# Middle stages of a hybrid encoder step: the low parts of weight blocks cut on VectorE, the query norm sums placed inside the projection, and the third norm's transposes placed between output products

## The chip, the cores and the metric

The kernel runs on one core of one Trainium2 chip. The metric is the device time of one execution in microseconds (us). Three runs of the kernel before took 1071.44, 1071.8 and 1072.5 us; their median is 1071.8 us. TensorE (PE) multiplies, VectorE (DVE), ScalarE (ACT) and GpSimd (POOL) do the rest, and SyncE (SP) issues all DMAs.

## The reference, cut to what matters

One layer runs for 640 tokens: a prompt of 512 and eight samples of 16. The change touches the end of the mixer, the memory cross-attention and the start of the ConvFFN.

```python
x = x + jnp.concatenate([y_a, y_b, y_c], axis=-1) @ w_mix_out

h = rmsnorm(x, norm_mem_g)
qm = rmsnorm((h @ w_mq).reshape(B, T, MEM_HEADS, MEM_DH), mq_norm_g)
s = jnp.einsum('bthd,bnhd->bhtn', qm, mem_k) * (MEM_DH ** -0.5)
p = jax.nn.softmax(s, axis=-1)
om = jnp.einsum('bhtn,bnhd->bthd', p, mem_v).reshape(B, T, MEM_W)
x = x + om @ w_mo

h = rmsnorm(x, norm_ffn_g)
gt, ffn_buf_new = causal_dwconv(h @ w_gate, ffn_buf, ffn_conv_w)
x = x + (jax.nn.silu(gt) * (h @ w_up)) @ w_down
```

The memory's keys and values of the prompt come from `m = rmsnorm(mem)`, `m @ w_mk` and `m @ w_mv`; those of the samples are read from caches. D_MODEL is 1024, MEM_HEADS 4, MEM_DH 128, 256 memory rows, D_FF 2816.

## The kernel before, in words

All engines run programs written out by hand, each strictly in its order, and wait for each other on semaphores. Tokens are cut into five tiles of 128 rows (`NT` = 5); tile 4 (`PT`) holds the samples.

**Products in three parts.** A large product multiplies a high and a low part: high weight by high activation, high by low, low by high. Weights come in blocks of 1 MB (128 x 2048 numbers), numbered in the order of their use: 16 and 17 the second half of `w_mix_out`, 18 and 19 `w_mk`, 20 and 21 `w_mq`, 22 and 23 `w_mv`, 24 and 25 `w_mo`, then `w_gate` (26, 28, ...) and `w_up` (27, 29, ...) in turn. `load_w(i)` on SP brings block i into `wraw[i % 3]` once block i-3 is used up (`passed`). `cut_hi(i)` on ACT copies it into `whi[i % 2]` once block i-2 is used up. `cut_lo(i)` writes the low part over `wraw`; it stands in the program of VectorE (line 1808) or of GpSimd (line 1210), as `on_dve(i)` says, and `lo_cut` is PE's wait for it. Before the change GpSimd cuts blocks 19 and 21 to 27 of the middle stages.

**Norms.** For tile n, ACT sums squares (`square_rows`, line 1636) and forms the root, VectorE scales the rows (`scaled_rows`, line 2156) into one of two buffers `xn`, PE transposes them (`turn_rows`, line 505), ACT copies the high part (`norm_hi`, line 1335) and VectorE the low part (`norm_lo`, line 1818).

**Memory attention.** The two query blocks give `qm`; four heads' squares (`q_square`, line 2204) are summed by PE with a matrix of ones (line 924), ACT forms the roots, VectorE scales (line 2209). For each tile i PE forms the scores (`mem_scores`, line 938; `sample_scores`, line 976, for the samples), VectorE the maxima (`soft_max`, lines 2220 and 2223), ACT the exponentials (line 1696), VectorE divides by the sums (`soft_norm`, lines 2228 and 2230), PE transposes (`mem_probs`, line 948), ACT copies out, PE multiplies by the values (`mem_values`, line 961; `sample_values`, line 991), ACT and VectorE split the result (`om_part`), PE multiplies by `w_mo` (`mem_out`, lines 487 to 489), VectorE adds to the residual (`add_mem`, line 2149). PE's loop staggers these:

```python
for i in range(NT):
    if i + 1 < PT:
        mem_scores(i + 1)
    elif i + 1 == PT:
        sample_scores()
    if i == 0:
        memory_rows("mv", B_MV, 1, mv_banks)
    mem_probs(i)
    if i >= 1:
        mem_values(i - 1)
    if i >= 2:
        mem_out(i - 2)
```

PE writes into eight PSUM banks taken in a ring (`take`); a bank is taken again only when its reader has freed it. In this loop the scores of tile 2 take the two banks of the `w_mv` product.

The FFN starts with `across_half`, lines 420 to 422: the first gate block on tokens 0 to 319, then the last transposes, the first up block, and both on tokens 320 to 639.

## Time and profile before

| what | value |
|---|---|
| median of three runs | 1071.8 us |
| time of the profiled execution | 1075.18 us |
| its span (first to last instruction) | 1073.5 us |
| busy: PE, DVE, ACT, POOL | 1020.7, 534.2, 393.6, 117.3 us |
| PE idle from 400 to 640 us of the span, sum of the listed waits | 20.1 us |
| TensorE clock granted, mean | 0.984 |

The busy time of PE overlaps its own pipelining, so its share says only that PE rarely waits. All waits of PE from 400 to 640 us of the span lie between 463 and 606 us: these are the stages that the change edits. The granted clock is a share of 2.4 GHz; 0.50 is the lower level, 1.2 GHz.

### The profile page before, as it was taken

What the parts mean: (1) busy time and instruction counts of PE and PEld (TensorE: products, weight loads), DVE (VectorE), ACT (ScalarE), POOL (GpSimd) and SP (SyncE); (2) the same over time, 40 slices, a digit from 0 to 9 for tenths busy, and PEclk for the clock granted to TensorE, in tenths of its full rate; (3) what the DMA queues carried; (4) which work ended last, traced back from release to release, by engine and by line L of the source; (5) the groups of instructions that cost most, each with busy time, mean ns of one, the idle gap of its engine ahead of it and who ended that gap; (6) DMA issues with size and microseconds to landing.
All of it is one profiled execution on the core that took longest, in us unless ns stands there. A gap on an engine that the chain in (4) does not pass through costs nothing.

```text
span 1073.5 us, 16639 instructions
## 1 busy us (share of the span) xinstructions
PE 1020.7 (95%) x7027; PEld 913.8 (85%) x7027; DVE 534.2 (50%) x944; ACT 393.6 (37%) x729; POOL 117.3 (11%) x118
## 2 busy tenths in 40 slices
PE   4999999999999979989889799999999999999998
PEld 3888888897888857869678799999999999888887
DVE  5323686775756463662553444444444445533531
ACT  5413344438633434443544422222222223433320
POOL 0500000000373332013310300000000000000000
PEclk8999999999999989999989899999999999999999
DMA  7342233121101234342631222211222222212231
GB/s 265 124 151 89 79 118 119 41 81 44 40 2 52 70 126 158 107 138 98 230 104 59 79 80 79 77 61 64 77 79 79 79 80 86 79 59 79 79 108 49
DMA packets 73513, 98.44 MB, mean 92 GB/s; under 512 B 2528, under 2 KB 53856, under 8 KB 73312
## 3 DMA queue, kind: packets, MB, share of 16 engines
q1 hardware_dynamic: 73440, 97.39, 27.4%
q8 instruction: 56, 0.92, 0.4%
q14 instruction: 17, 0.14, 0.0%
HBM read 89.65 MB, written 7.73 MB: 91 GB/s over the span
## 4 chain that ended last, share of the span: by engine, by line
PE 82%; DVE 9%; ACT 5%; POOL 2%; issue 2%; DMA 0%; SPq 0%; DVEq 0%; ACTq 0%
PE bank L402 30%; PE bank L461 6%; PE bank L463 6%; PE bank L462 6%; PE bank L434 3%; PE bank L436 3%; PE bank L435 3%; PE bank L487 2%; PE bank L489 2%; PE bank L488 2%; PE bank L712 1%; DVE wlo L1808 1%; PE bank L516 1%; PE bank L420 1%; POOL lmb L1281 1%
## 5 line engine op out<-in xcount | busy, mean ns | idle before, releaser
L402 PE MATMUL bank<-hhi,whi 128*128 128x320 f32 x736 | 221.7, 309 | 0.1
L402 PE MATMUL bank<-hlo,whi 128*128 128x320 f32 x736 | 221.6, 309 | 0.0
L1325 ACT ACTIVATE whi<-wraw 128x2048 fp32r<-128x2048 f32 (+1 forms) x59 | 111.4, 1888 | 188.5 <-PE bank L402 95.8
L402 PE MATMUL bank<-hhi,wlo 128*128 128x320 f32 x736 | 167.6, 309 | 0.0
L1808 DVE TENSOR_TENSOR wlo<-wraw,whi 128x2048 fp32r<-128x2048 f32 (+1 forms) x50 | 112.3, 2246 | 89.5 <-ACT whi L1325 89.5
L402 PEld LDWEIGHTS bank<-hhi,whi 128*128 128x128 f32 x736 | 138.2, 188 | 0.4 <-issue 0.3
L402 PEld LDWEIGHTS bank<-hlo,whi 128*128 128x128 f32 x736 | 138.1, 188 | 0.1
L402 PEld LDWEIGHTS bank<-hhi,wlo 128*128 128x128 f32 x736 | 123.0, 188 | 0.0
L434 PE MATMUL bank<-hhi,whi 128*128 128x320 f32 x352 | 114.2, 324 | 0.7 <-DVE gT L1861 0.7
L436 PE MATMUL bank<-hhi,wlo 128*128 128x320 f32 x352 | 108.8, 309 | 0.0
L435 PE MATMUL bank<-hlo,whi 128*128 128x320 f32 x352 | 108.7, 309 | 0.0
L461 PE MATMUL bank<-whi,hhi 128*128 128x512 f32 x200 | 79.1, 396 | 6.2 <-DVE hlo L1827 6.2
L462 PE MATMUL bank<-wlo,hhi 128*128 128x512 f32 x200 | 78.8, 394 | 0.0
L463 PE MATMUL bank<-whi,hlo 128*128 128x512 f32 x200 | 78.8, 394 | 0.0
L434 PEld LDWEIGHTS bank<-hhi,whi 128*128 128x128 f32 x352 | 66.2, 188 | 4.0 <-issue 3.7
L1374 ACT ACTIVATE cb<-bank 128x320 f32<-128x320 f32 x34 | 14.9, 438 | 147.7 <-PE bank L402 110.0
L435 PEld LDWEIGHTS bank<-hlo,whi 128*128 128x128 f32 x352 | 66.2, 188 | 1.7 <-issue 1.4
L436 PEld LDWEIGHTS bank<-hhi,wlo 128*128 128x128 f32 x352 | 66.1, 188 | 0.0
L1210 POOL TENSOR_TENSOR wlo<-wraw,whi 128x2048 fp32r<-128x2048 f32 x10 | 45.8, 4586 | 147.7 <-ACT whi L1325 147.7
L2308 DVE TENSOR_TENSOR act<-act,bank 128x320 f32<-128x320 f32 x44 | 19.5, 484 | 71.1 <-PE bank L402 71.1
L461 PEld LDWEIGHTS bank<-whi,hhi 128*128 128x128 f32 x200 | 38.2, 191 | 14.6 <-issue 6.7
L1868 DVE COPY fcst<-cb 128x2 f32<-128x2 f32 x22 | 3.7, 170 | 83.5 <-ACT cb L1377 83.3
(369 smaller groups left out, 1800.4 us busy)
## 6 DMA issues: line engine op xcount, KB each, us to landing
wraw<-in_w_in SPq DMA_DIRECT2D x14, 1024.0 KB, 5.3
wraw<-in_w_gate SPq DMA_DIRECT2D x11, 1024.0 KB, 5.2
wraw<-in_w_up SPq DMA_DIRECT2D x11, 1024.0 KB, 5.3
wraw<-in_w_down SPq DMA_DIRECT2D x10, 1024.0 KB, 5.0
kTs<-in_cache_sb_k SPq DMA_DIRECT2D x8, 512.0 KB, 5.4
vraw<-in_cache_sb_v SPq DMA_DIRECT2D x8, 512.0 KB, 6.0
wraw<-in_w_mix_out SPq DMA_DIRECT2D x4, 1024.0 KB, 5.0
kmT<-in_cache_mem_k SPq DMA_DIRECT2D x8, 512.0 KB, 5.8
```

The source lines that it names most:

```text
L402: ins = T.matmul(bank[bs[h]][:, 0:HALF], w[:, k, c * P:(c + 1) * P], a[:, k, h * HALF:(h + 1) * HALF], start=(k == 0 and w is wh and a is hi),
L434: T.matmul(o, wh[:, k, cs], hhi[:, k, hs], start=(k == 0), stop=False)
L435: T.matmul(o, wh[:, k, cs], hlo[:, k, hs], start=False, stop=False)
L436: ins = T.matmul(o, wl[:, k, cs], hhi[:, k, hs], start=False, stop=(k == KD - 1))
L461: T.matmul(o, hi[:, t * P:(t + 1) * P], wh[:, kk, :], start=(k == 0), stop=False)
L462: T.matmul(o, hi[:, t * P:(t + 1) * P], wl[:, kk, :], start=False, stop=False)
L463: ins = T.matmul(o, lo[:, t * P:(t + 1) * P], wh[:, kk, :], start=False, stop=(k == nk - 1))
L487: T.matmul(bank[b][:, :], hi[:, tt], wh[:, kk, :], start=(k + kk == 0), stop=False)
L488: T.matmul(bank[b][:, :], hi[:, tt], wl[:, kk, :], start=False, stop=False)
L1210: G.tensor_tensor(wv(wlo, i), wv(wraw, i), wv(whi, i).bitcast(F32), ALU.subtract)\
L1325: V(wv(whi, i), wv(wraw, i), ACT.Copy).then_inc(s["w_hi_ready"], 1)
L1808: V.tensor_tensor(wv(wlo, i), wv(wraw, i), wv(whi, i).bitcast(F32), ALU.subtract)\
```

## The change

- All weight blocks from 16 on are cut on VectorE; GpSimd keeps blocks 14 and 15 only, and takes over the clearing of the two tiles `pz` from VectorE.
- Both `w_mk` blocks are cut before tile 4 of the second norm is squared and scaled.
- The query norm sums of heads 0 and 1 stand between the two halves of the second query block, that of head 2 behind it, and that of head 3 inside the first `w_mv` product.
- VectorE, not ACT, scales the memory values out of PSUM (`memv`).
- The first gate block (26) gets a high buffer of its own, `whi_gate`, in the place of two of the samples' key tiles; it is loaded before the last of the samples' value tiles and cut in iteration 3 of the loop.
- The third norm's transposes stand between output products; the output product of tile 4 is split into its two column halves.

```diff
         def on_dve(i):
-            return i < B_OUT[0][0] or i in B_OUT[1] or i in (B_MK[0], B_MQ[0]) or i >= B_GU[1][0]
+            return i not in B_OUT[0]
...
+            if t is whi and i == B_GU[0][0]:
+                return whi_gate[:, :].rearrange("p (k c) -> p k c", k=nk)
...
-            across(("mq", 1), B_MQ[1], hhi, hlo)
+            across(("mq", 1), B_MQ[1], hhi, hlo, cs=(0,))
...
+            query_sums(0)
+            query_sums(1)
+            across(("mq", 1), B_MQ[1], hhi, hlo, cs=(1,))
+            query_sums(2)
...
+            memory_rows("mv", B_MV, 0, mv_banks, behind=lambda kk: query_sums(3) if kk == 0 else None)
...
             sample_values()
+            turn_norm3(0)
+            turn_sample_values()
             mem_out(3)
-            turn_norm3(0)
             turn_norm3(1)
-            turn_sample_values()
+            mem_out(PT, 0)
             turn_norm3(2)
-            mem_out(PT)
+            mem_out(PT, 1)
             turn_norm3(3)
...
+            load_w(B_GU[0][0])
             filled(sp, ("ms", PT, 1))
             load_mem_v(7)
-            for i in range(B_GU[0][0], B_DN[0][0] + 2):
+            for i in range(B_GU[0][1], B_DN[0][0] + 2):
...
-            for i in range(B_MK[1], B_GU[1][0]):
-                if i != B_MQ[0]:
-                    cut_lo(i)
+            passed(pool, B_MV[1])
+            for n in range(2):
+                ins = G.memset(pz[n][:, :, :, :], 0.0)
+            ins.then_inc(s["pz_ready"], 1)
...
-                if i == 0:
-                    for t in range(2):
-                        b = filled(e, ("mv", 0, t))
-                        V(memv[:, t, :], bank[b][:, :], ACT.Copy, scale=stat[:, 2, t:t + 1]).then_inc(bank_free[b], 1)
-                    cut_hi(B_MO[1][0])
...
+                if i == 3:
+                    cut_hi(B_GU[0][0])
...
+            cut_lo(B_MV[1])
             soft_max(0)
+            cut_lo(B_MO[0][0])
             soft_norm(0)
...
+                        for t in range(2):
+                            b = filled(dve, ("mv", 0, t))
+                            V.tensor_scalar(memv[:, t, :], bank[b][:, :], stat[:, 2, t:t + 1], None, ALU.mult)\
+                                .then_inc(bank_free[b], 1)
...
+                if i == 3:
+                    cut_lo(B_GU[0][0])
```

On PE, behind the second query block, the program before has the transposes of the memory keys, then the sums of the four heads in a row (`sqM`), then the first `w_mv` product:

```order
L402 MATMUL bank<-hhi,wlo_173 128x320 x2
L918 MATMUL bank<-ident,mkout 128x128 x8
L924 MATMUL bank<-sqM_166,ones 128x320 x2
L924 MATMUL bank<-sqM_167,ones 128x320 x2
L924 MATMUL bank<-sqM_166,ones 128x320 x2
L924 MATMUL bank<-sqM_167,ones 128x320 x2
L895 MATMUL bank<-whi_176,mhi 128x512
```

In the changed program the same place of PE reads as follows; the rows left out are the second half of the query block (39 rows) and the first six rows of the `w_mv` product:

```order
L923 MATMUL bank<-ident,mkout 128x128 x8
L930 MATMUL bank<-sqM_166,ones 128x320 x2
L930 MATMUL bank<-sqM_167,ones 128x320 x2
L405 MATMUL bank<-hhi,whi_178 128x320
...
L405 MATMUL bank<-hhi,wlo_173 128x320 x2
L930 MATMUL bank<-sqM_166,ones 128x320 x2
L898 MATMUL bank<-whi_177,mhi 128x512
...
L930 MATMUL bank<-sqM_167,ones 128x320 x2
L898 MATMUL bank<-whi_177,mhi 128x512
```

Two heads' sums have moved ahead of half a query block, and one behind a quarter of the next product. On VectorE, from the copies of the samples' queries (`qz`) to the second tile's softmax, before:

```order
L2241 COPY qz_200<-qm 128x16x16
L2220 TENSOR_REDUCE mstat<-bank 128x2 x2
L2223 TENSOR_SCALAR mstat<-mstat 128x4
L2228 RECIPROCAL mstat<-mstat 128x4
L2230 TENSOR_SCALAR probs_195<-probs_195,mstat 128x256 x4
L2220 TENSOR_REDUCE mstat<-bank 128x2 x2
L2223 TENSOR_SCALAR mstat<-mstat 128x4
L2228 RECIPROCAL mstat<-mstat 128x4
```

And in the changed program, on the same engine and at the same place:

```order
L2263 COPY qz_201<-qm 128x16x16
L1828 TENSOR_TENSOR wlo_175<-wraw_172,whi_178 128x2048
L2242 TENSOR_REDUCE mstat<-bank 128x2 x2
L2245 TENSOR_SCALAR mstat<-mstat 128x4
L1828 TENSOR_TENSOR wlo_173<-wraw_170,whi_177 128x2048
L2250 RECIPROCAL mstat<-mstat 128x4
L2252 TENSOR_SCALAR probs_196<-probs_196,mstat 128x256 x4
L2242 TENSOR_REDUCE mstat<-bank 128x2 x2
L2245 TENSOR_SCALAR mstat<-mstat 128x4
L2279 TENSOR_SCALAR memv<-bank,stat 128x512 x2
L2250 RECIPROCAL mstat<-mstat 128x4
```

Two cuts (`wlo`) and the scaling of the memory values have come into the softmax chain of VectorE. On SP's DMA queue, from the seventh of the samples' value tiles on, before:

```order
L1156 DMA mkraw_135<-in_cache_mem_v 128x2x512
L1169 DMA out_p_mem_v<-memv 128x2x512
L1156 DMA mkraw_136<-in_cache_mem_v 128x2x512
L1067 DMA wraw_172<-in_w_gate 128x8x256
L1067 DMA wraw_170<-in_w_up 128x8x256
```

The same stretch of SP's queue in the changed program:

```order
L1169 DMA mkraw_135<-in_cache_mem_v 128x2x512
L1182 DMA out_p_mem_v<-memv 128x2x512
L1080 DMA wraw_172<-in_w_gate 128x8x256
L1169 DMA mkraw_136<-in_cache_mem_v 128x2x512
L1080 DMA wraw_170<-in_w_up 128x8x256
```

The first gate block has passed the last value tile, and with it the wait for the samples' scores.

## Rows read from the trace of the kernel before

**Rows 1.** The page: busy time of the engines, and DMA time to landing

```profile
PE 1020.7 (95%) x7027; PEld 913.8 (85%) x7027; DVE 534.2 (50%) x944; ACT 393.6 (37%) x729; POOL 117.3 (11%) x118
...
wraw<-in_w_up SPq DMA_DIRECT2D x11, 1024.0 KB, 5.3
```

**Rows 2.** PE's waits, 400 to 640 us: total, times, longest

```profile
PE bank L948 <- DVE probs L2230: 3.8, 2, 2.4
PE bank L924 <- DVE sqM L2204: 2.2, 2, 2.0
```

**Rows 3.** Stretches: busy us (instructions) per engine, PE clock, DMA share, GB/s

```profile
474.40:482.30 7.90, 7.90 (x33) 6.77 (x34) 4.65 (x5) 3.00 (x3) 0.00 (x0) 0.80 0.22 87
523.90:553.00 29.10, 22.45 (x113) 19.27 (x112) 19.31 (x30) 13.16 (x34) 11.49 (x3) 0.88 0.61 217
605.10:612.00 6.90, 6.87 (x30) 6.90 (x31) 2.17 (x5) 1.83 (x4) 4.78 (x1) 0.60 0.09 27
```

**Rows 4.** Timeline of PE, 470 to 606 us: start, duration, idle before

```profile
474.40 1.97 PE L505 MATMUL bank<-ident,xn 128*128 128x128 f32 x8 [4.09 <-DVE xn L2156]
...
523.87 3.61 PE L938 MATMUL bank<-memkT,qm 128*128 128x256 f32 x16
527.13 0.58 PE L895 MATMUL bank<-whi,mhi 128*128 128x512 f32 x1
...
538.32 3.16 PE L938 MATMUL bank<-memkT,qm 128*128 128x256 f32 x8 [2.85 <-ACT memv L1728]
...
553.00 0.47 PE L487 MATMUL bank<-whi,omhi 128*128 128x512 f32 x1
...
562.25 1.09 PE L948 MATMUL bank<-ident,probs 128*128 128x128 f32 x8
563.18 1.95 PE L961 MATMUL bank<-probT,memv 128*128 128x128 f32 x16
564.89 0.47 PE L487 MATMUL bank<-whi,omhi 128*128 128x512 f32 x1
...
570.47 1.04 PE L948 MATMUL bank<-ident,probs 128*128 128x128 f32 x8
...
578.67 3.70 PE L991 MATMUL bank<-mkraw,pz 128*32 128x128 f32 x128
...
592.83 1.28 PE L505 MATMUL bank<-ident,xn 128*128 128x128 f32 x8 [2.60 <-DVE xn L2156]
...
605.13 0.61 PE L420 MATMUL bank<-hhi,whi 128*128 128x320 f32 x1 [3.27 <-POOL wlo L1210]
```

**Rows 5.** Timeline of POOL: a memset, and two stretches of cuts

```profile
342.86 0.95 POOL L1288 MEMSET apart_w<- 128x1024 f32 x1 [17.85 <-PE bank L436]
...
468.73 4.53 POOL L1210 TENSOR_TENSOR wlo<-wraw,whi 128x2048 fp32r<-128x2048 f32 x1 [39.57 <-ACT whi L1325]
...
521.76 9.11 POOL L1210 TENSOR_TENSOR wlo<-wraw,whi 128x2048 fp32r<-128x2048 f32 x2 [16.71 <-ACT whi L1325]
```

**Rows 6.** Timeline of DVE, 459 to 543 us

```profile
459.11 1.28 DVE L2156 SCALAR_TENSOR_TENSOR xn<-xres,stat,gmem 128x1024 f32<-128x1024 f32 x1 [1.90 <-issue]
...
462.15 2.29 DVE L1808 TENSOR_TENSOR wlo<-wraw,whi 128x2048 fp32r<-128x2048 f32 x1 [0.56 <-ACT whi L1325]
...
470.37 3.98 DVE L2156 SCALAR_TENSOR_TENSOR xn<-xres,stat,gmem 128x1024 f32<-128x1024 f32 x1
...
526.52 4.38 DVE L2223 TENSOR_SCALAR mstat<-mstat 128x4 f32<-128x4 f32 x1
...
533.18 1.14 DVE L2230 TENSOR_SCALAR probs<-probs,mstat 128x256 f32<-128x256 f32 x4
534.23 1.28 DVE L2220 TENSOR_REDUCE mstat<-bank 128x2 f32<-128x512 f32 x2
535.55 0.17 DVE L2223 TENSOR_SCALAR mstat<-mstat 128x4 f32<-128x4 f32 x1
...
542.24 3.02 DVE L2223 TENSOR_SCALAR mstat<-mstat 128x4 f32<-128x4 f32 x1
```

**Rows 7.** Timeline of ACT: the second w_mk block's high part

```profile
466.75 1.90 ACT L1325 ACTIVATE whi<-wraw 128x2048 fp32r<-128x2048 f32 x1
```

More of the change, by code:

```diff
@@ L885, in _, with memory_rows @@
             pe.wait_ge(s["mem_lo"], 1)
-            def memory_rows(name, blks, part, bs):
+            def memory_rows(name, blks, part, bs, behind=lambda kk: None):
                 lo_cut(pe, blks[part])
@@ L899, in memory_rows @@
                             done(ins, (name, 0, t))
+                    if kk < 3:
+                        behind(kk)
                 if part == 0:
@@ L1000, in turn_sample_values, with mem_out @@
                 done(ins, ("om", PT))
-            def mem_out(n):
+            def mem_out(n, *halves):
                 evacuated(pe, ("om", n))
-                for half in range(2):
+                for half in halves or range(2):
                     rows_tiles("mo", half, B_MO[half], lambda h, k: (omhi[:, k, :], omlo[:, k, :]), (n,))
@@ L1668, in _, with query_roots @@
             cut_hi(B_MV[0])
[L1669 to L1675 removed]
+            def query_roots(h):
                 if h >= 2:
@@ L2257, in _ @@
                 if i == 1:
-                    passed(dve, B_MV[1])
-                    for n in range(2):
-                        ins = V.memset(pz[n][:, :, :, :], 0.0)
-                    ins.then_inc(s["pz_ready"], 1)
+                    cut_lo(B_MO[1][0])
                 if i == 2:
```

51 lines of the change are left out of this document (32 added, 19 removed).

## Prediction

> **What bounds the kernel now.** I read the page first: PE is busy 95% of the span, VectorE 50% and GpSimd 11% [rows 1]. So time can be won only where PE waits or where its clock is down, and a few us of extra work on VectorE cost nothing unless PE waits for them. The view of PE's waits says where that is: from 400 to 640 us it idles 20.1 us, all between 463 and 606. The timeline of PE places the waits. There are four places. Before the last transposes of the second norm PE stands 4.09 us [rows 4]. Within the query norm sums it stands 2.2 us [rows 2]. Between the first scores (523.87) and the first output product (553.00) it stands twice for normalised probabilities, 3.8 us together [rows 2], and 2.85 us for the banks of the memory values [rows 4]. Before the FFN it stands 2.60 us for scaled rows and 3.27 us for the cut of the gate block [rows 4]. The stretches show the second part of the price: after each of these, the granted clock is below 1, so that some of the matmuls run at 1.2 instead of 2.4 GHz: 0.80 over 7.9 us, 0.88 over 29.1 us, 0.60 over 6.9 us [rows 3]. PE had stood still before each fall.
>
> The timelines of VectorE and GpSimd name the cause of most of it. A cut takes 2.29 us on VectorE [rows 6] and 4.53 us on GpSimd [rows 5]. And while GpSimd cuts, VectorE's instructions between SBUF tiles stand: the scaled rows take 3.98 us at 470.37, where 1.28 is normal, and the four numbers of `mstat` take 4.38 and 3.02 us, where 0.17 is normal [rows 6]. Each overlaps a GpSimd cut: 468.73 to 473.26, and 521.76 to 530.87 [rows 5].
>
> **The change part by part.**
>
> *Second norm, last tile.* The load of the second `w_mk` block lands at 466.75, when ACT starts on its high part, done at 468.65 [rows 7]. Now ACT does that before the squares of tile 4, and VectorE cuts for 2.29 us, to about 470.95, then scales for 1.28 us, to about 472.3. Today the transposes start at 474.40: 2.1 us won. Idle of about 2.0 us stays, because the squares now queue behind the load. What the clock does then is open. If it stays up, the 7.9 us at 0.80 give back up to 7.9 x 0.20 = 1.6 us; if not, nothing. I take the middle, 0.8. The first query block's cut, next on VectorE, then ends some 0.5 us before PE asks for it, because its high part waits on ACT behind both halves of this norm.
>
> *Query norm sums.* Heads 0 and 1 are squared long before the half block that now follows them; heads 2 and 3 have half a projection (7 us, a quarter of the 28 us that both blocks take) and 1.4 us of the `w_mv` product as cover. The 2.2 us of waiting go [rows 2]. Without the cover they would be back. The work is the same number of matmuls.
>
> *From the first scores to the first output product.* Today 29.13 us pass (523.87 to 553.00). The work at full clock, from start to start of rows: two tiles' scores 3.26 (523.87 to 527.13), a product of 24 matmuls 5.58 (564.89 to 570.47), three rounds of transposes of 0.93 (562.25 to 563.18), two of values of 1.71 (563.18 to 564.89), two more tiles of scores 3.26, in sum 18.3 us [rows 4]. So if nothing waited, 10.8 us would go. Does VectorE keep up? In these 18.3 us it has three maxima (1.28 + 0.17), three divisions (0.18 + 1.14) [rows 6], two evacuations of `memv` of 0.68, one low part of 0.69, and about three cuts of 2.29: some 17 us, 90% full. Going step by step from the first scores: scores in PSUM at 1.8 us, VectorE free of the `w_mv` cut at 1.6, maxima at 3.3, exponentials 1.9 us, `w_mo` cut beside them to 5.5, probabilities at 6.9; PE is in the `w_mv` product until 9.1, so this round is covered by 2 us. `memv` is scaled at 9.9, just when PE asks for those banks after its transposes. Second probabilities at 11.7 against PE's 11.6; third at 16.5 against 16.0; the second `w_mo` cut is done at 21.0 against 21.9. I leave 0.6 us for the two thin ones: 10.2 us won. Of that, 6.65 us is idle time and the rest is clock.
>
> *Clearing `pz` on GpSimd.* Two memsets of about 0.95 us [rows 5], released by the end of the `w_mv` product, beside the second tile's division. They take 1.8 us off VectorE. Nothing in the trace shows a memset beside that work. Bounds: nothing, and 1.9 us if they hold VectorE as the cuts do. A memset reads no SBUF tile, so it is nearer to nothing; I take 0.3. The Trainium skill, "SBUF — State Buffer", section "Who interferes with whom", has one exclusive port pair for GpSimd and VectorE's two-port forms, whoever comes first, for the whole instruction, `tensor_scalar` among them. By that rule the memsets could hold the division for up to their length, which is the upper bound above; the rows on cuts agree with it.
>
> *Before the FFN.* Today 26.46 us pass from the samples' values (578.67) to the first gate matmul (605.13). The work: 3.7 for the values, four transposes of 0.93, 0.5 for the turned sample values, two output products of 5.58, in sum 19.1 us [rows 4]; so 7.4 us go if nothing waits. Going through: scaled rows 0 and 1 are ready before the loop's end, row 2 about 5 us before its turn, row 3 about 2 us. The gate block, loaded from about 10 us after the first scores, is cut some 20 us before its use. The up block is loaded when the first half of tile 4's output product ends, lands 5.3 us later [rows 1], and is cut after the last scaled rows, 10.3 us after its issue; PE reaches it after 12.4 us. It is covered by 2 us. The first half of the gate block runs at 0.60 today for 6.9 us: 2.8 us come back, since no idle precedes it [rows 3].
>
> Sum: 2.1 + 0.8 + 2.2 + 10.2 - 0.3 + 7.4 + 2.8 = 25.2 us. The FFN behind is the same stream, so all of it should reach the end. The profiled execution took 1075.18 us, span 1073.5, and should take about 1050.0. It lay 3.4 us above the median of 1071.8, which I take as what the profile adds to both; so 1071.8 - 25.2 = **1046.6 us**.
>
> **The rivals.**
>
> *VectorE becomes the bound in the softmax loop.* Every cut stands between a maximum and a division or ahead of a maximum. If the handovers take longer than I set, three cuts (6.9 us) and `memv` (1.4) come onto PE's path, and the clock stays down as today (about 3.5 us). For it: 90% full, covers of 0.1 and 0.5 us. Against it: VectorE's 19.31 busy us of that stretch hold 7.1 us of standing for GpSimd (4.38 + 3.02 less 2 x 0.17) [rows 3, 6]. It would give 1046.6 + 11.8 = 1058 us. Chance 0.13.
>
> *The waits shrink but the clock is not given back, or the up block comes late.* A 2 us hole remains at the second norm, behind a 0.9 us one; short waits of 0.5 to 1 us at the third and fourth probabilities could keep the clock down as in the 29 us today. Loses 3.5 + 0.8, or for the up block 1 to 3 us and part of the 2.8: about 1051 to 1053. Chance 0.16.
>
> *Slower than before.* The gate block's high part waits on ACT in iteration 3, ahead of the samples' transposed probabilities, for its load and for the samples' scores. If that load came late, everything on ACT stood behind it: the probabilities' copies, the third tile's `om_part`, and so PE. It would have to be more than 30 us late to eat the gain and the cover (it is issued some 18 us before the wait, with 5.3 us to land [rows 1]). Delays of that size give over 1075. Chance 0.02.
>
> *The change does nothing here.* The waits would have to reappear at full size behind other causes, in a kernel with VectorE at 50%: within 0.2% of before, 1070 to 1074. Chance 0.01.
>
> *More than I sum.* Clock at full everywhere and the second norm's idle gone: 20.1 us of waits and 10 us of clock, 1041.7. Chance 0.04 beyond 1043.
>
> **How the numbers follow.** The forecast, 1043 to 1049.5, has 0.64. With the case of the clock it reaches 1053, in sum 0.80, so the range is 1042 to 1054; the rest lies mostly above. 0.2% (2.1 us) is about what a measurement can tell from no change. Every case but two, which hold 0.03, is faster; I leave a little more for what I have not seen: faster 0.95, same 0.02, slower 0.03.
>
> **What would show it.** In the changed profile: no GpSimd cut after 400 us; `xn` never above 1.3 us and `mstat` at 0.17; transposes of the second norm about 2 us earlier; no wait at the sums; first scores to first output product in about 19 us, at a clock near 1; no wait of PE on the gate block, and its first half at 0.147 us a matmul. I am wrong if PE waits for `probs`, `memv` or `wlo` for more than 2 us in sum in that stretch, if the division shows a stall beside the memsets, or if the FFN that follows grows.

## The result

The changed kernel took 1047.16 us in the median of four runs (1045.9 to 1048.69). Four runs of the kernel before had a median of 1072.15 us (1071.44 to 1074.93). The ratio is 0.9757, with a 95% interval of 0.9731 to 0.9783: the kernel is 2.4% faster. 1046.6 was predicted.

The page of the changed kernel, its span, busy times and granted clock per slice, answers to [rows 1]:

```profile
span 1046.6 us, 16640 instructions
...
PE 1011.6 (97%) x7027; PEld 907.0 (87%) x7027; DVE 538.9 (51%) x952; ACT 392.0 (37%) x727; POOL 82.3 (8%) x112
...
PEclk8999999999999998999999999999999999999999
```

PE is busy 9 us less although it issues the same 7027 matmuls: they run at the higher clock. GpSimd loses 35 us, VectorE gains only 5. The eight cuts it took over are 18 us of work (8 x 2.29), and it no longer stands while GpSimd cuts: behind the change its scaled rows take 1.27 to 1.28 us and the four numbers of `mstat` 0.17. The waits of PE from 400 to 640 us (total, times, longest), which answer to [rows 2], were 20.1 us before and are now 2.3. One of them lies outside the stages that the change edits, 0.36 us at 429.22 before and 0.33 at 430.25 now (`mxlo`), so 19.7 us, not 20.1, lay between 463 and 606.

```profile
PE bank L898 <- DVE wlo L1828: 0.9, 1, 0.9
PE bank L508 <- DVE xn L2176: 0.6, 1, 0.6
PE bank L960 <- DVE probs L2252: 0.5, 2, 0.3
PE bank L464 <- POOL mxlo L1317: 0.3, 1, 0.3
```

Stretches, with the columns of [rows 3]; the last three figures of a row are PE's clock, the DMA share and GB/s. The first row is the whole loop from the first scores to the first output product. The clock was 0.88 in that loop before and is 1.00 now.

```profile
517.19:536.61 19.42, 18.92 (x114) 16.39 (x112) 15.35 (x30) 11.93 (x31) 1.84 (x2) 1.00 0.89 301
...
460.00:480.00 20.00, 18.51 (x93) 15.28 (x93) 14.61 (x14) 11.63 (x15) 0.00 (x0) 1.00 0.53 185
...
580.00:600.00 20.00, 20.00 (x142) 19.99 (x141) 6.95 (x10) 6.74 (x13) 0.00 (x0) 1.00 0.21 71
```

The places of [rows 4] on PE's timeline now:

```profile
465.60 0.47 PE L898 MATMUL bank<-whi,mhi 128*128 128x512 f32 x1 [0.88 <-DVE wlo L1828]
...
471.93 1.09 PE L508 MATMUL bank<-ident,xn 128*128 128x128 f32 x8 [0.61 <-DVE xn L2176]
...
517.19 3.61 PE L950 MATMUL bank<-memkT,qm 128*128 128x256 f32 x16
...
529.15 1.09 PE L960 MATMUL bank<-ident,probs 128*128 128x128 f32 x8 [0.28 <-DVE probs L2252]
...
533.97 1.09 PE L960 MATMUL bank<-ident,probs 128*128 128x128 f32 x8 [0.22 <-DVE probs L2252]
...
536.61 0.48 PE L490 MATMUL bank<-whi,omhi 128*128 128x512 f32 x1
...
580.80 0.39 PE L423 MATMUL bank<-hhi,whi_gate 128*128 128x320 f32 x1
```

No wait stands before the first gate matmul (580.80). Cut into stages by the start of their first matmul, each difference below is one of two such rows. The kernels of the next section, most of which take parts of the change back, are in the same table, so that each part can be read in its own column. The last column is the rest of the span behind the first gate matmul; since that half block runs first there, the clock at the gate shows in it.

| kernel | first `w_mk` to first query block | to key transposes | to first scores | to first output product | to sample values | to first gate matmul | all six | rest of the span |
|---|---|---|---|---|---|---|---|---|
| before | 17.70 | 28.15 | 13.43 | 29.13 | 25.67 | 26.46 | 140.54 | 468.37 |
| changed | 12.74 | 21.12 | 17.73 | 19.42 | 25.65 | 18.54 | 115.20 | 465.80 |
| e1_cuts_alone | 16.32 | 28.15 | 14.56 | 20.00 | 25.65 | 23.90 | 128.58 | 466.26 |
| e2_cuts_back | 16.59 | 21.11 | 17.74 | 21.64 | 26.83 | 18.53 | 122.44 | 466.42 |
| e3_sums_back | 12.57 | 28.17 | 14.85 | 19.42 | 25.65 | 18.53 | 119.19 | 465.85 |
| e4_gate_late | 12.54 | 21.13 | 17.73 | 19.42 | 25.66 | 20.23 | 116.71 | 466.33 |
| e5_turns_back | 12.62 | 21.12 | 17.73 | 19.42 | 25.65 | 22.98 | 119.52 | 465.81 |
| e6_memv_act | 12.79 | 21.12 | 17.73 | 19.42 | 25.67 | 18.53 | 115.26 | 465.82 |
| e7_pz_vector | 12.72 | 21.13 | 17.74 | 18.72 | 25.65 | 18.54 | 114.50 | 465.87 |
| e8_pz_later | 12.85 | 21.12 | 17.73 | 19.80 | 25.66 | 18.54 | 115.70 | 465.89 |
| e9_squares_first | 12.00 | 21.11 | 17.74 | 19.41 | 25.66 | 18.53 | 114.45 | 465.85 |
| e10_pz_at_cut | 13.15 | 21.11 | 17.74 | 18.72 | 25.65 | 18.54 | 114.91 | 465.86 |
| e11_pool_busy | 12.92 | 21.13 | 17.74 | 25.01 | 25.66 | 18.53 | 120.99 | 465.85 |
| e12_both | 12.06 | 21.12 | 17.73 | 18.72 | 25.66 | 18.53 | 113.82 | 465.84 |

From the second column on, stages that an edit doesn't touch repeat within 0.03 us (the last column within 0.1), so this table tells apart what the run times, with their 1 to 3 us of scatter, don't. It rests on one profiled execution of each kernel. The first column scatters by 0.6 where it isn't edited (12.54 to 13.15). Moved work must be seen in it: half a query block (7 us) left the second column for the third in the changed kernel.

### The profile page after: what moved, and what is told of

Read it like the earlier page. It is cut to its first block, busy times and chain, and to the rows that moved or that the text cites. A ratio compares the mean times of both kernels' runs of the same rounds, so it can differ in the third digit from the quotient of the medians.

```text
span 1046.6 us, 16640 instructions
## 1 busy us (share of the span) xinstructions
PE 1011.6 (97%) x7027; PEld 907.0 (87%) x7027; DVE 538.9 (51%) x952; ACT 392.0 (37%) x727; POOL 82.3 (8%) x112
## 3 DMA queue, kind: packets, MB, share of 16 engines
q1 hardware_dynamic: 73440, 97.39, 27.9%
## 4 chain that ended last, share of the span: by engine, by line
PE 84%; DVE 7%; ACT 4%; POOL 2%; issue 1%; DMA 1%; SPq 0%; DVEq 0%; ACTq 0%
PE bank L405 31%; PE bank L464 6%; PE bank L465 6%; PE bank L466 6%; PE bank L437 4%; PE bank L439 3%; PE bank L438 3%; PE bank L492 2%; PE bank L490 2%; PE bank L491 2%; PE bank L715 1%; DVE wlo L1828 1%; PE bank L519 1%; POOL lmb L1295 1%; PE bank L423 1%
## 5 line engine op out<-in xcount | busy, mean ns | idle before, releaser
L1828 DVE TENSOR_TENSOR wlo<-wraw,whi 128x2048 fp32r<-128x2048 f32 (+1 forms) x57 | 128.4, 2252 | 95.8 <-ACT whi L1342 95.8
L465 PEld LDWEIGHTS bank<-wlo,hhi 128*128 128x128 f32 x200 | 38.3, 191 | 7.9
```

The lines of the kernel that those rows point to most:

```text
L465: T.matmul(o, hi[:, t * P:(t + 1) * P], wl[:, kk, :], start=False, stop=False)
L1828: V.tensor_tensor(wv(wlo, i), wv(wraw, i), wv(whi, i).bitcast(F32), ALU.subtract)\
```

## The experiments

The run times, each beside runs of the kernel before on the same chip:

| kernel | median, us | ratio to before | 95% interval |
|---|---|---|---|
| e1_cuts_alone | 1061.18 | 0.9875 | 0.9835 to 0.9915 |
| e2_cuts_back | 1054.79 | 0.9817 | 0.9769 to 0.9866 |
| e3_sums_back | 1050.40 | 0.9777 | 0.9737 to 0.9817 |
| e4_gate_late | 1049.25 | 0.9763 | 0.9722 to 0.9803 |
| e5_turns_back | 1051.62 | 0.9809 | 0.9794 to 0.9824 |
| e6_memv_act | 1046.48 | 0.9765 | 0.9751 to 0.9780 |
| e7_pz_vector | 1046.42 | 0.9765 | 0.9750 to 0.9780 |
| e8_pz_later | 1047.07 | 0.9770 | 0.9753 to 0.9786 |
| e9_squares_first | 1046.44 | 0.9764 | 0.9749 to 0.9778 |
| e10_pz_at_cut | 1045.68 | 0.9757 | 0.9741 to 0.9774 |
| e11_pool_busy | 1052.12 | 0.9818 | 0.9803 to 0.9832 |
| e12_both | 1045.98 | 0.9760 | 0.9746 to 0.9775 |

The theory: each stage had its own wait, on its own cause, and each part of the change removes one; the cuts on VectorE take away GpSimd's holding of VectorE, and the orders take away the rest. The rivals: that one part does nearly all of it, and that VectorE, or the clock, is the bound in the softmax loop after all.

**The cuts alone (e1_cuts_alone).** The kernel before, with the cuts on VectorE at places that fit its order, and nothing else.

```diff
         def on_dve(i):
-            return i < B_OUT[0][0] or i in B_OUT[1] or i in (B_MK[0], B_MQ[0]) or i >= B_GU[1][0]
+            return i not in B_OUT[0]
...
-            for i in range(B_MK[1], B_GU[1][0]):
-                if i != B_MQ[0]:
-                    cut_lo(i)
...
                 scaled_rows("norm2", n, 7, gmem, xn2)
+                if n == PT:
+                    cut_lo(B_MK[1])
...
+            cut_lo(B_MV[1])
             soft_max(0)
+            cut_lo(B_MO[0][0])
             soft_norm(0)
...
             norm_lo("norm3", 2)
+            cut_lo(B_GU[0][0])
             add_mem(4)
```

> The kernel before with one part of the change alone: all cuts of blocks 19 and 21 to 27 on VectorE, none on GpSimd; PE's order, the norm sums, memv on ScalarE and the place of the gate block's load and high part are as before. Theory (the slow and blocking cuts on GpSimd were the main cost): second norm 2 us earlier, the VectorE instructions that stood 2.7 to 4.2 us stand no more, so the stretch from the first scores to the first output product shrinks by about 8 us, the gate block's wait of 3.3 us to about 1, some clock comes back; gain 12 to 16 us, about 1058 us. Rival (the placement of PE's work and the early gate block pay, the cuts only ride along): gain under 6 us, over 1066 us.

It took 1061.18 us. The six stages shrink by 11.96 us and the rest of the span by 2.11, just under the 12 to 16 us that I expected. Its four largest waits of PE:

```profile
PE bank L505 <- DVE xn L2153: 4.0, 2, 2.6
PE bank L895 <- DVE wlo L1805: 2.0, 2, 1.1
PE bank L924 <- DVE sqM L2204: 2.0, 1, 2.0
PE bank L420 <- DVE wlo L1805: 1.0, 1, 1.0
```

The loop falls to 20.00 by the cuts alone. The waits for the sums (`sqM`) and for scaled rows (`xn`, 1.4 and 2.6) stay, and the clock falls behind them. So the cuts alone are worth about half of the whole; the other half needs the orders.

**All but the cuts (e2_cuts_back).** The changed kernel with GpSimd cutting the blocks it cut before, and `pz` cleared on VectorE.

```diff
         def on_dve(i):
-            return i not in B_OUT[0]
+            return i < B_OUT[0][0] or i in B_OUT[1] or i in (B_MK[0], B_MQ[0]) or i >= B_GU[1][0]
...
-            passed(pool, B_MV[1])
-            for n in range(2):
-                ins = G.memset(pz[n][:, :, :, :], 0.0)
-            ins.then_inc(s["pz_ready"], 1)
+            for i in range(B_MK[1], B_GU[1][0]):
+                if i != B_MQ[0]:
+                    cut_lo(i)
```

> The changed kernel with the cuts of blocks 19 and 21 to 27 given back to GpSimd, in the same order as before, and pz cleared on VectorE; everything else stays changed (norm sums, transposes, gate buffer, memv on VectorE). Theory: the stalls of VectorE come back (xn and mstat at 3 to 4.4 us), loss of 12 to 16 us against the changed kernel, about 1060 us, all of it before the first output product; the stretch before the FFN stays short, since the early gate block hides even a 4.5 us cut. Rival: loss under 5 us, below 1052 us.

It took 1054.79 us: 18.10 us off the six stages and 1.95 off the rest. Against the changed kernel it loses 7.2 us in the stages, where I had expected 12 to 16, and 1.18 of it lies behind the first output product, where I had expected none. Neither my theory nor its rival (a loss under 5 us) had the size. VectorE's and then GpSimd's timeline show the holding once more:

```profile
525.69 3.20 DVE L2247 TENSOR_SCALAR probs<-probs,mstat 128x256 f32<-128x256 f32 x4
...
560.65 4.58 DVE L2175 SCALAR_TENSOR_TENSOR xn<-xres,stat,gffn 128x1024 f32<-128x1024 f32 x1
```

```profile
518.84 9.10 POOL L1224 TENSOR_TENSOR wlo<-wraw,whi 128x2048 fp32r<-128x2048 f32 x2 [13.55 <-ACT whi L1341]
...
559.57 4.57 POOL L1224 TENSOR_TENSOR wlo<-wraw,whi_gate 128x2048 fp32r<-128x2048 f32 x1 [14.59 <-ACT whi_gate L1341]
```

A division takes 3.20 for 1.14, scaled rows 4.58 for 1.28. In the loop that costs only 2.2 us more than on VectorE (21.64 against 19.42), and the clock is 1.00 there (523 to 545 us). That the new order has more cover is my reading; no run takes its parts there one by one. The halves don't simply add: 11.96 and 18.10 make 30.1, where both together give 25.34. In the loop they overlap, since the cuts alone win 9.13, the rest alone 7.49 and both 9.71. In the second norm they need each other: 1.38 and 1.11 alone, 4.96 together. The first rival falls, except in the loop, where either half does most of it.

**The sums back together (e3_sums_back).**

```diff
-            across(("mq", 1), B_MQ[1], hhi, hlo, cs=(0,))
+            across(("mq", 1), B_MQ[1], hhi, hlo)
...
-            query_sums(0)
-            query_sums(1)
-            across(("mq", 1), B_MQ[1], hhi, hlo, cs=(1,))
-            query_sums(2)
-            for g in range(2):
-                take(("mqn", 3, g))
+            for h in range(HEADS):
+                query_sums(h)
...
-            memory_rows("mv", B_MV, 0, mv_banks, behind=lambda kk: query_sums(3) if kk == 0 else None)
+            memory_rows("mv", B_MV, 0, mv_banks)
```

> The changed kernel with the four heads' query norm sums back in a row behind the whole second query block, on PE and on ScalarE. Theory: PE waits again for the squares of heads 2 and 3, 2.0 to 2.5 us in sum, and the clock stays at 1 there as it did before: 1049 to 1050 us. Rival (the sums were no cost because a later wait would swallow them): 1047 us and a wait further on that shrinks by as much.

It took 1050.40 us. The second and third column together are 43.02 against 38.85, 4.17 us more; the six stages 3.99. PE's timeline, then the stretch around it:

```profile
509.15 1.37 PE L930 MATMUL bank<-sqM,ones 128*128 128x320 f32 x4 [1.96 <-DVE sqM L2220]
...
510.75 2.50 PE L930 MATMUL bank<-sqM,ones 128*128 128x320 f32 x4 [0.23 <-DVE sqM L2220]
```

```profile
509.00:515.00 6.00, 5.62 (x16) 3.81 (x16) 2.96 (x5) 4.01 (x8) 0.00 (x0) 0.72 0.58 231
```

The 2.2 us of [rows 2] are back (1.96 + 0.23), and here the clock fell behind them, to 0.72. In the kernel before it had stayed up at the same place after the same wait. That is most of the other 2 us (0.28 x 6.0 = 1.7), and it is what I had not expected: I had the clock stay up, as before.

**The gate block late (e4_gate_late).** Block 26 without a high buffer of its own: loaded behind the last value tile, and cut behind the scaled rows.

```diff
             _, nk, n = blocks[i]
-            if t is whi and i == B_GU[0][0]:
-                return whi_gate[:, :].rearrange("p (k c) -> p k c", k=nk)
...
-            load_w(B_GU[0][0])
             filled(sp, ("ms", PT, 1))
             load_mem_v(7)
-            for i in range(B_GU[0][1], B_DN[0][0] + 2):
+            for i in range(B_GU[0][0], B_DN[0][0] + 2):
...
             norm_lo("norm3", 2)
+            cut_lo(B_GU[0][0])
             add_mem(4)
```

> The changed kernel without the gate block's own buffer and early cuts: load behind the samples' last value tile, high part after the first half of tile 4's output product, low part next on VectorE. The transposes between output products stay. Theory: PE waits about 1.5 to 2 us for the low part before the first gate matmul; whether the clock falls after so short a wait decides between a loss of 2 us (1049) and of up to 5 us (1052). Rival (the gate wait was only GpSimd's slowness): no wait, 1047 us.

It took 1049.25 us. The last stage is 1.69 longer and the rest 0.53. PE waits 1.45 at the gate, and the clock stays up. PE's timeline, and the stretch from there:

```profile
581.37 0.38 PE L421 MATMUL bank<-hhi,whi 128*128 128x320 f32 x1 [1.45 <-DVE wlo L1822]
```

```profile
581.30:590.00 8.70, 8.60 (x58) 8.19 (x59) 6.15 (x9) 6.02 (x11) 0.00 (x0) 1.00 0.27 93
```

So the early gate block is worth some 1.7 us once the cut is on VectorE (2.2 with the 0.53 behind it, whose cause wasn't looked for). The 3.27 us wait of [rows 4] was for GpSimd's cut; with the cut on VectorE, in the order before, it is 1.00 (e1).

**The transposes back (e5_turns_back).** The order of the kernel before between the output products, with the third tile's addition on VectorE where that order needs it.

```diff
             sample_values()
-            turn_norm3(0)
-            turn_sample_values()
             mem_out(3)
+            turn_norm3(0)
             turn_norm3(1)
-            mem_out(PT, 0)
+            turn_sample_values()
             turn_norm3(2)
-            mem_out(PT, 1)
+            mem_out(PT)
             turn_norm3(3)
```

> The changed kernel with the third norm's transposes and the samples' values in their old places behind tile 3's output product, and that of tile 4 in one piece; VectorE's order there as before; the gate block stays early. Theory: PE waits about 2.6 us for the scaled rows of tile 2 and the clock falls behind it as before (0.84 over 14.9 us): loss of 3 to 5 us, 1050 to 1052 us. Rival (the wait was caused by what stood before it and is gone with it): 1047 us.

It took 1051.62 us; the last stage is 22.98, 4.44 more. PE's timeline and the stretch behind that wait:

```profile
575.57 1.09 PE L508 MATMUL bank<-ident,xn 128*128 128x128 f32 x8 [2.60 <-DVE xn L2175]
```

```profile
575.50:590.00 14.50, 14.43 (x78) 12.96 (x79) 7.89 (x10) 6.55 (x14) 0.00 (x0) 0.88 0.46 146
```

It is the 2.60 us wait of [rows 4], with GpSimd doing nothing. That wait was a matter of order, as VectorE's timeline shows:

```profile
571.88 1.29 DVE L1837 TENSOR_TENSOR hlo<-bank,hhi 128x512 fp32r<-128x512 f32 x2 [0.38 <-ACT hhi L1351]
573.63 0.69 DVE L2258 TENSOR_TENSOR omlo<-bank,omhi 128x512 fp32r<-128x512 f32 x1 [0.46 <-ACT omhi L1732]
574.24 1.27 DVE L2175 SCALAR_TENSOR_TENSOR xn<-xres,stat,gffn 128x1024 f32<-128x1024 f32 x1
```

The rows that PE waits for are those of tile 2 (`turn_norm3(2)`). Their addition and their root were done by 564.0. But on VectorE their scaling stands behind the low part of tile 0 and that of the samples' output, and both of these need transposes that PE reaches only at 570.62 and 572.36, just ahead. In the changed kernel PE transposes tile 0 right behind the samples' values, and tile 2 is scaled 7.4 us before its turn (569.02 and 576.39). The clock fell behind the wait (0.88 over 14.5 us, 1.7 us).

**The memory values on ACT again (e6_memv_act).** This takes 1.4 us off VectorE in the loop. If VectorE were the bound, PE should gain by it.

```diff
+                if i == 0:
+                    for t in range(2):
+                        b = filled(e, ("mv", 0, t))
+                        V(memv[:, t, :], bank[b][:, :], ACT.Copy, scale=stat[:, 2, t:t + 1]).then_inc(bank_free[b], 1)
...
-                    if i == 0:
-                        for t in range(2):
-                            b = filled(dve, ("mv", 0, t))
-                            V.tensor_scalar(memv[:, t, :], bank[b][:, :], stat[:, 2, t:t + 1], None, ALU.mult)\
-                                .then_inc(bank_free[b], 1)
```

> The changed kernel with the memory values scaled out of PSUM by ScalarE again. Theory: ScalarE comes to them only after the second tile's exponentials and then to the transposed probabilities 1.2 us later; PE waits 0.7 to 1.5 us for the two banks, VectorE is 1.4 us freer; 1047.5 to 1048.5 us. Rival (VectorE at 90% is the bound in this loop): the 1.4 us taken off VectorE make it faster, 1046 us or less.

The loop takes 19.42 us, as with it on VectorE, and the run 1046.48. PE now waits 0.4 for `memv` and no longer for `probs` (0.5 before). So where the values are scaled makes no difference in the new order. I had expected a wait of 0.7 to 1.5 us and a loss; and since one wait takes the place of another, this run alone doesn't test whether VectorE is the bound.

**`pz` cleared on VectorE (e7_pz_vector).** Now VectorE has 1.8 us more to do, and GpSimd nothing.

```diff
-            passed(pool, B_MV[1])
-            for n in range(2):
-                ins = G.memset(pz[n][:, :, :, :], 0.0)
-            ins.then_inc(s["pz_ready"], 1)
...
                     cut_lo(B_MO[1][0])
+                    passed(dve, B_MV[1])
+                    for n in range(2):
+                        ins = V.memset(pz[n][:, :, :, :], 0.0)
+                    ins.then_inc(s["pz_ready"], 1)
```

> The changed kernel with pz cleared on VectorE (1.8 us) behind the second w_mo cut, none on GpSimd. Theory (the memsets on GpSimd held VectorE's division for 0.7 us): the second division is back at 1.14 us, PE's wait of 0.28 us before the second transposes goes; the 1.8 us on VectorE are covered; time within 0.5 us of the changed kernel. Rival (VectorE is the bound): the 1.8 us show on PE ahead of the fourth transposes.

The loop is shorter: 18.72 us, and both waits for `probs` are gone. VectorE's own memsets come at 535.74, 1.6 us behind the loop's end (534.17), and the stage there is no longer for them (25.65 us). VectorE's and GpSimd's timelines of the changed kernel show why the loop is shorter:

```profile
522.42 1.14 DVE L2252 TENSOR_SCALAR probs<-probs,mstat 128x256 f32<-128x256 f32 x4
...
527.24 1.85 DVE L2252 TENSOR_SCALAR probs<-probs,mstat 128x256 f32<-128x256 f32 x4
```

```profile
526.33 1.84 POOL L1321 MEMSET pz<- 128x1024 f32 x2 [96.14 <-PE bank L900]
```

The second division overlaps the memsets (526.33 to 528.17) and takes 0.71 us longer than the first. In e7 the same division takes 1.15. So the memsets cost the loop 0.70 us. In run time that isn't told apart from nothing: 1046.42 against 1047.16, with intervals that overlap.

**The memsets elsewhere (e8_pz_later, e10_pz_at_cut).** Both were meant to bring the memsets beside a cut on VectorE, to see whether they hold that too. In e8 they wait for the first memory values' product, in e10 for its evacuation.

```diff
             passed(pool, B_MV[1])
+            filled(pool, ("om", 0))
             for n in range(2):
```

```diff
             passed(pool, B_MV[1])
+            evacuated(pool, ("om", 0))
             for n in range(2):
```

> The changed kernel with GpSimd's two memsets held until the first output tile of the attention is in PSUM, beside VectorE's second w_mo cut (a subtraction of two SBUF tiles). If a memset on GpSimd holds only VectorE's one-input scalings, the cut stays at 2.29 us, the second division is back at 1.14 us and PE's 0.28 us wait goes; if it holds any work between SBUF tiles, the cut takes 3 to 4 us or the memsets wait for it. Time within 0.5 us of the changed kernel either way.

> The changed kernel with GpSimd's two memsets released when VectorE has freed the first output tile's bank, so that they run beside VectorE's second w_mo cut (two SBUF inputs), not beside a scaling. If memsets hold only VectorE's one-input scalings, the cut starts at once after its high part and lasts 2.29 us, and no scaling is stretched; if they hold the cut too, it lasts or waits 1 to 2 us longer. PE's wait of 0.28 us before the second transposes goes in both cases; time 1046 to 1047 us.

In e8 the product ended earlier than I had placed it, and the memsets fell on the third division, so it didn't test what I had written down; e10 does. GpSimd's row, then VectorE's, then PE's:

```profile
529.37 1.99 POOL L1322 MEMSET pz<- 128x1024 f32 x2 [101.61 <-PE bank L973]
```

```profile
529.80 2.22 DVE L2253 TENSOR_SCALAR probs<-probs,mstat 128x256 f32<-128x256 f32 x4
```

```profile
532.07 1.09 PE L960 MATMUL bank<-ident,probs 128*128 128x128 f32 x8 [1.10 <-DVE probs L2253]
```

The third division takes 2.22, PE waits 1.10 for it, and the loop is 19.80, 1.08 more than without memsets there. In e10 they met the cut, GpSimd's row and VectorE's:

```profile
532.51 1.84 POOL L1322 MEMSET pz<- 128x1024 f32 x2 [104.30 <-DVE omlo L2260]
```

```profile
533.50 2.29 DVE L1829 TENSOR_TENSOR wlo<-wraw,whi 128x2048 fp32r<-128x2048 f32 x1 [1.11 <-ACT whi L1343]
```

The cut takes its 2.29 and the loop 18.72, as without memsets. So in these runs memsets held VectorE's scaling of one SBUF tile and not its subtraction of two. The Trainium skill, "SBUF — State Buffer", section "Who interferes with whom", says the same: an instruction of VectorE with two SBUF inputs contends only with one of GpSimd that reads SBUF, while `tensor_scalar` in its two-port form contends with any. By that rule the price of the memsets hangs on which instruction they meet, and e7, e8 and e10 bear it out with 0.70, 1.08 and 0.

**GpSimd made busy (e11_pool_busy).** Four multiplications in which GpSimd reads SBUF, placed in the loop; nothing reads what they write, and nothing of the computation is left out.

```diff
+            for i in (B_MV[1], B_MO[0][0]):
+                pool.wait_ge(s["w_hi_ready"], i + 1)
+                for n in range(2):
+                    link(G.tensor_tensor(lmask[:, :, :], lmask[:, :, :], lmask[:, :, :], ALU.mult))
             passed(pool, B_MV[1])
```

> The changed kernel, all cuts on VectorE in time, with four added multiplications on GpSimd of two SBUF tiles of 128 x 896 (about 2 us each by the 4.53 us for 2048 columns), two released by the high part of block 23 and two by that of block 24; nothing reads their results. It takes the lateness of GpSimd's cuts away and leaves only their holding of VectorE. If holding is the larger part of what the cuts cost in the softmax loop, VectorE's instructions stretch by 4 to 8 us in sum and the loop from the first scores to the first output product grows from 19.4 by 2 us or more. Rival (lateness was the cost): the loop stays within 0.5 us of 19.4.

It took 1052.12 us, and the loop 25.01, 5.59 more. GpSimd's timeline, first the four in one row, then three of them by themselves; then VectorE's:

```profile
515.10 11.06 POOL L1322 TENSOR_TENSOR lmask<-lmask 128x896 f32<-128x896 f32 x4 [86.45 <-ACT whi L1346]
...
515.10 3.79 POOL L1322 TENSOR_TENSOR lmask<-lmask 128x896 f32<-128x896 f32 x1 [86.45 <-ACT whi L1346]
518.96 3.68 POOL L1322 TENSOR_TENSOR lmask<-lmask 128x896 f32<-128x896 f32 x1
522.72 1.68 POOL L1322 TENSOR_TENSOR lmask<-lmask 128x896 f32<-128x896 f32 x1
```

```profile
518.82 2.28 DVE L1832 TENSOR_TENSOR wlo<-wraw,whi 128x2048 fp32r<-128x2048 f32 x1
...
521.23 6.11 DVE L2256 TENSOR_SCALAR probs<-probs,mstat 128x256 f32<-128x256 f32 x4
```

The division stands for 5 us (6.11 for 1.14) with GpSimd's multiplications, which lie on nobody's path. The cut at 518.82 isn't stretched, though GpSimd's four lie across it: there GpSimd stood. Its third and fourth multiplications take 1.68 us each, its first two 3.79 and 3.68, and each of these two began 0.05 and 0.14 us behind the start of a cut on VectorE (515.05 and 518.82, 2.29 and 2.28 us). The Trainium skill, "SBUF — State Buffer", section "Who interferes with whom", has the shared ports as an exclusive lock, which for VectorE's two-port forms whoever issues first keeps for its whole instruction. The held division agrees with it (6.11 us), and here the two cuts, which have two SBUF inputs, held GpSimd in the same way. So the holding alone, with no cut moved, lengthens the loop by 5.6 us, part of it as clock (0.66 over 526 to 536 us). That is what these four cost in the new order, not a share of the 9.7 us of the change: GpSimd's real cuts cost 2.2 in the same loop (e2).

**Squares first (e9_squares_first).** In the second norm ACT and VectorE take tile 4's squares and scaling ahead of the second `w_mk` block's cut, as the kernel before did; the cut stays on VectorE.

```diff
-                    cut_hi(B_MK[1])
                 square_rows(n, 7, "out", junk2)
+                if n == PT:
+                    cut_hi(B_MK[1])
...
+                scaled_rows("norm2", n, 7, gmem, xn2)
                 if n == PT:
                     cut_lo(B_MK[1])
-                scaled_rows("norm2", n, 7, gmem, xn2)
                 if n >= 1:
                     norm_lo("norm2", n - 1)
```

> The changed kernel with the squares and the scaling of the second norm's tile 4 put back ahead of the second w_mk block's high and low parts (all on ScalarE and VectorE). My reading of the changed trace: the squares wait for that block's load (0.6 us of PE idle left). Then this wait goes, the low part is done just in time for its product, and the stage is 0.6 us shorter: 12.1 instead of 12.7 us from the first w_mk product to the query block. Rival (the order of the two cuts was needed): PE waits 0.5 to 1.5 us for the low part instead, and the stage is as long or longer.

The first stage takes 12.00 us, 0.74 less than in the changed kernel, and PE's wait for `xn` is gone. So this reordering of the change is a small loss. It also shows what had been the gain. VectorE in e1_cuts_alone, which has the same order of cuts and squares, and then in e9:

```profile
468.04 1.29 DVE L1815 TENSOR_TENSOR hlo<-bank,hhi 128x512 fp32r<-128x512 f32 x2 [4.12 <-ACT hhi L1332]
469.24 1.27 DVE L2153 SCALAR_TENSOR_TENSOR xn<-xres,stat,gmem 128x1024 f32<-128x1024 f32 x1
```

```profile
465.55 1.29 DVE L2177 SCALAR_TENSOR_TENSOR xn<-xres,stat,gmem 128x1024 f32<-128x1024 f32 x1 [1.90 <-issue]
467.30 2.29 DVE L1829 TENSOR_TENSOR wlo<-wraw,whi 128x2048 fp32r<-128x2048 f32 x1 [0.46 <-ACT whi L1342]
```

In e1, as before the change, VectorE does tile 3's low part (`hlo`) ahead of tile 4's scaling, and waits 4.12 us with it for ACT, which is at the `w_mk` block. In e9, as in the changed kernel, the low part stands behind the scaling. The move is in the change's diff:

```diff
                 if n == PT:
-                    norm_lo("norm2", n - 1)
+                    cut_lo(B_MK[1])
                 scaled_rows("norm2", n, 7, gmem, xn2)
-                if 1 <= n < PT:
+                if n >= 1:
                     norm_lo("norm2", n - 1)
```

In this stage the orders of e1 and e9 differ in nothing else, so the move of `norm_lo` is what tells 16.32 us from 12.00: PE's waits of 1.39 and 1.11 us in e1, and the fall of the clock that followed (0.78 over 472.7 to 480 us, 1.6 us).

**Both repairs (e12_both).** The edits of e7 and e9 together, which the two point to.

> The changed kernel with pz cleared on VectorE and the squares of tile 4 first: the two small waits that the changed trace still shows (0.6 us and 0.5 us) are gone together. From the first w_mk product to the first gate product 113.9 to 114.1 us instead of 115.2; about 1046 us. Rival: less than 0.5 us is won, since one wait moves into the next.

The six stages take 113.82 us, the shortest of all, 1.38 less than in the changed kernel; 0.68 of it is in the first stage, 0.70 in the loop. In the first stage e9 and e12 (12.00 and 12.06) lie below all kernels with the changed order there (12.54 to 13.15). PE's only waits left from 400 to 640 us are 0.9 for the first `w_mk` cut and 0.4 for `mxlo`. Its run time, 1045.98, isn't told apart from 1047.16: the interval of its ratio, 0.9746 to 0.9775, holds 0.9757. That it is faster is shown by its profile's stages, not by its times.

## Why the prediction was right

Every term came where the prediction had it, and most sizes were near. In us, each with the rows of the table of stages:

| term | predicted | measured |
|---|---|---|
| second norm, waits and clock | 2.1 + 0.8 | 17.70 - 12.74 = 4.96 |
| query norm sums | 2.2 | 41.58 - 38.85 = 2.73 |
| first scores to first output product, with the memsets | 10.2 - 0.3 | 29.13 - 19.42 = 9.71 |
| before the FFN | 7.4 | 26.46 - 18.54 = 7.92 |
| clock of the first gate half block | 2.8 | 468.37 - 465.80 = 2.57 |
| sum | 25.2 | 27.9 |

**Second norm: the term that was mis-sized.** The step "the load of the second `w_mk` block lands at 466.75" was wrong. I took the start of ACT's instruction for the landing. Its row [rows 7] names no releaser and follows the root of tile 4's squares: ACT had been busy, and by the changed kernel's row below the block had then been there for about 1.3 us. In the changed kernel ACT does stand for the load, on its timeline:

```profile
466.44 1.92 ACT L1342 ACTIVATE whi<-wraw 128x2048 fp32r<-128x2048 f32 x1 [3.31 <-DMA wraw<-in_w_mk]
```

That is 0.84 us behind PE's first `w_mk` matmul (465.60), where the prediction had it 2.16 behind (466.75 from 464.59): 1.32 us earlier. The transposes moved from 9.81 us behind that matmul (474.40 from 464.59) to 6.33 (471.93 from 465.60): 3.48 us won, the predicted 2.1 and this 1.3. The idle left is 0.61 us, not 2.0, and the clock stays at 1.00, which gives the other 1.5 us, the upper end of my bounds (1.6) and not their middle. The prediction's working also had nothing on the move of tile 3's low part on VectorE, without which the stage would have won little, as e1 shows. The cuts ahead of the squares, on which I rested the term, cost 0.7 (e9).

**Sums.** The wait is gone and each of its 2.2 us with it; 0.5 more came than the wait, which no single row shows. "Without the cover they would be back" held in e3, but it priced only the wait: there the clock fell too, and the cost was 4.0.

**The loop.** The total was right to 0.2 us (9.71 for 9.9), but by misses that cancel. Without memsets beside a division, and without any wait, the loop takes 18.72 us (e7, e10), where I had summed 18.3. The 0.6 us that I left for the second and third probabilities weren't needed: PE waits 0.28 and 0.22 for them in the changed kernel, but both waits are gone in e7, so they belong to the memsets. The 0.3 for the memsets was too little, 0.70, well inside the bounds of 0 and 1.9; of the prediction's three signs of being wrong this one came, a division that stalls beside the memsets (1.85 us for 1.14), while the other two did not (0.5 us of waits in that stretch, and an FFN that didn't grow). And my reason for the 0.3 ("a memset reads no SBUF tile, so it is nearer to nothing") was wrong for the division. The rule that the prediction set beside it was right for it (e8), and e10 shows for which instruction my reason holds.

**Before the FFN.** The last stage is 18.54 us, and the work that I summed was 19.1: no wait is left. Two parts are shown apart by taking each back, 4.4 for the order (e5) and 1.7 for the early gate block (e4). The 1.8 that is left of the 7.9 is put down to the cut of the gate block on VectorE, which gave 2.56 by itself in e1; the parts needn't add up. The up block isn't waited for.

**The gate's clock.** 2.6 for 2.8.

**The rivals.** VectorE isn't the bound of the loop. It is busy 15.35 of 19.42 us, 79% where I had summed 90%, and in the changed kernel it stands 3.8 us in it for PE and ACT, ahead of `memv`, of the third division and of the last cut:

```profile
525.62 1.44 DVE L2279 TENSOR_SCALAR memv<-bank,stat 128x512 f32<-128x512 f32 x2 [0.65 <-PE bank L900]
...
532.56 0.18 DVE L2250 RECIPROCAL mstat<-mstat 128x4 f32<-128x4 f32 x1 [2.06 <-ACT probs L1718]
...
535.75 2.29 DVE L1828 TENSOR_TENSOR wlo<-wraw,whi 128x2048 fp32r<-128x2048 f32 x1 [1.11 <-ACT whi L1342]
```

Taking 1.4 us off it (e6) changes nothing. Nor did the clock stay down: it is 1.00 in the three stretches of the changed kernel above. The slower case, a late gate load that blocks ACT, is not seen. The case of "more than I sum" came in part: the clock is up in all of these stages, and the idle of the second norm is down to 0.61 us.

**From the sum to the median.** Two more misses cancel most of the 2.7 us by which the sum is short. PE reaches the first `w_mk` matmul at 465.60 in the changed profile and at 464.59 in that of before, so 26.9 us show in the spans (1073.5 and 1046.6). The work up to there is the same in all kernels here, yet it starts between 463.20 and 465.62: scatter of the stages before. Part of it is seen: in the changed profile the clock is 0.50 from 338.0 to 341.4 us, with PE busy throughout, which costs some 1.7 us; in that of before it is 1.00 from 337.0 to 341.5. The rest of the scatter stays open. And the profiled execution was 3.4 us above the median before (1071.8) but 1.5 above it after (1048.69 against 1047.16). I had taken 3.4 for both, as what the profile adds. The granted clocks on record say otherwise: the mean was 0.984 in the profiled execution of before and 0.987 in 18 of the 21 later runs of that kernel (1070.6 to 1073.4 us), and 0.003 of 1073.5 us is 3.2 us. So the profile that I read had some 3 us more of low clock than most executions have. Where, and so which term is too large by it, one profile doesn't show; the 27.9 of the table holds it. Between the medians lie 25.0 us. That the forecast was met within 0.6 us is to that extent luck.

## What to carry to other kernels

GpSimd work isn't free because GpSimd is idle. Its cuts and multiplications held VectorE here, and even its memsets held a division: look for VectorE instructions that take longer than usual, and price the work by what waits for those. Move a part of a change back by itself before you credit it: here the cuts that moved ahead of the squares cost 0.7 us, and it was a low part moved along with them that made room for the gain. Before you take the start of an instruction for the landing of its data, see whether its engine was idle; if the row names no releaser, the data may have been there for long. Before you subtract from a median what you read in one profile, compare its granted clock with that of the other runs. Where PE's clock has fallen behind a wait, an edit that closes the wait is worth more than the wait (here some 28 us for 18 us of idle, between the two profiles), and a small wait that is brought back can cost double.

## What the runs showed of the hardware

- **Equal waits, unequal clock.** After an idle of 1.96 to 1.97 us ahead of the third head's sums the granted clock stayed at 1.00 in the kernel before and fell in e1 (0.66 over 5 us) and e3 (0.72 over 6 us). After 0.88 and 0.61 us in the changed kernel and after 1.45 in e4 it stayed up; after 2.60 (e5, 0.88 over 14.5 us) and 2.89 us (e2, second norm, 0.77 over 7.3 us) it fell. In e1 it fell too behind two short ones, 1.39 and 1.11 us with 1.1 us of transposes between them (0.78 over 7.3 us). So a wait near 2 us may or may not cost its double here, and only the profile of that run says which.
- **Whoever comes first holds the other.** In e11 two GpSimd multiplications that began just behind a VectorE cut took 3.79 and 3.68 us, where 1.68 is normal, and the cuts kept their 2.29 and 2.28; a division that began while GpSimd was at work took 6.11 us for 1.14.
- **Very small instructions are held too.** In e2 the scaling of four columns of `mstat`, 0.17 us when nothing disturbs it, took 1.18 and 2.43 us beside GpSimd's cuts, as in [rows 6].
- **Memsets hold by kind.** 1.84 to 1.99 us of memsets on GpSimd lengthened a division of VectorE by 0.71 (the changed kernel) and 1.08 us (e8), and a cut by nothing (e10).
